# A stick-breaking attention layer: pairs of steps, 64-row tiles on TensorE, and subtractions moved to GpSimd

## What is computed

```python
h = rmsnorm(x, a_norm)                      # x: 2048 x 1024, float32
q, k, v, g = split(h @ w_in, 4)             # 16 heads of 64
z = q @ k.T / 8                             # t x s, only s < t counts
w[t, s] = sigmoid(z[t, s]) * prod(1 - sigmoid(z[t, j]) for s < j < t)
x = x + ((w @ v) * silu(g)) @ w_out
out = rmsnorm(x, final_norm)
```

## Time and profile before

| | us |
|---|---|
| median of 3 runs (1651.22 to 1652.89) | 1651.32 |
| the profiled execution | 1651.07 |
| its span, first to last instruction | 1649.3 |

### The profile page before, as it was taken

The page is one execution under the profiler, slowest core; times in us unless marked ns, Lnnn a source line. Parts: engine busy times, 40 slices in busy tenths (PEclk is TensorE's granted clock), DMA queues, the critical chain, the costliest instruction groups (busy, mean ns, idle before and its releaser), DMA issues.

```text
span 1649.3 us, 23497 instructions
## 1 busy us (share of the span) xinstructions
PE 1638.1 (99%) x8642; PEld 1376.1 (83%) x8642; DVE 1348.6 (82%) x1901; ACT 904.7 (55%) x1782; POOL 165.5 (10%) x200
## 2 busy tenths in 40 slices
PE   9999999999999999999999999999999999999998
PEld 7888878888888888888888888888888888888887
DVE  5536369989898999899998999898889899957874
ACT  6625245655665566656565655656566656743221
POOL 0020020110111011101110211012011101000000
PEclk9999999999999999999999999999999999999999
DMA  9858643343424252434333333425242424779722
GB/s 314 276 163 277 190 142 108 110 126 92 150 68 136 69 154 80 132 94 124 109 98 106 120 113 90 132 87 147 58 147 81 144 77 129 247 259 363 247 105 87
DMA packets 164370, 237.10 MB, mean 144 GB/s; under 512 B 49952, under 2 KB 91936, under 8 KB 164256
## 3 DMA queue, kind: packets, MB, share of 16 engines
q1 hardware_dynamic: 94912, 160.29, 31.5%
q10 hardware_dynamic: 69344, 75.32, 14.6%
HBM read 155.78 MB, written 79.76 MB: 143 GB/s over the span
## 4 chain that ended last, share of the span: by engine, by line
PE 96%; DMA 2%; ACT 1%; DVE 0%; POOL 0%; issue 0%; SPq 0%; DVEq 0%
PE proj_ps L764 31%; PE turn_ps L794 15%; PE o_ps L810 8%; PE o_ps L812 8%; PE z_ps L784 8%; PE z_ps L782 8%; PE proj_ps L713 5%; PE turn_ps L851 3%; PE o_ps L713 3%; PE turn_ps L713 3%; PE z_ps L851 3%; PE proj_ps L851 2%; PE o_ps L851 1%; DMA gate<-gate_cols 1%; POOL w_raw L697 0%; DMA w_raw<-in_w_qkg 0%
## 5 line engine op out<-in xcount | busy, mean ns | idle before, releaser
L1003 ACT ACTIVATE u<-z_ps 128x512 f32<-128x512 f32 (+3 forms) x640 | 341.6, 534 | 365.4 <-PE z_ps L784 362.3
L1236 DVE TENSOR_TENSOR_SCAN u<-u,u 128x512 f32<-128x512 f32 x384 | 492.1, 1281 | 0.0
L1241 DVE TENSOR_TENSOR r_turned_lo<-turn_ps,r_turned_hi 128x512 fp32r<-128x512 f32 (+3 forms) x640 | 380.9, 595 | 103.5 <-ACT r_turned_hi L1009 99.5
L1009 ACT ACTIVATE r_turned_hi<-turn_ps 128x512 fp32r<-128x512 f32 (+3 forms) x640 | 341.0, 533 | 96.7 <-PE turn_ps L794 45.2
L794 PE MATMUL turn_ps<-ident,u 128*128 128x128 f32 x2176 | 352.6, 273 | 0.0
L764 PE MATMUL proj_ps<-hT_hi,w_hi 128*128 128x512 f32 x768 | 317.9, 414 | 0.0
L764 PE MATMUL proj_ps<-hT_hi,w_lo 128*128 128x512 f32 x768 | 317.7, 414 | 0.0
L764 PE MATMUL proj_ps<-hT_lo,w_hi 128*128 128x512 f32 x768 | 317.5, 413 | 0.0
L794 PEld LDWEIGHTS turn_ps<-ident,u 128*128 128x128 f32 x2176 | 266.8, 140 | 54.5
L697 POOL TENSOR_SCALAR w_raw<-w_raw,a_norm_col 128x128 f32<-128x128 f32 x192 | 163.7, 871 | 1201.3 <-DMA w_raw<-in_w_qkg 1201.3
L784 PE MATMUL z_ps<-k_parts,q_swapped 128*128 128x512 f32 (+3 forms) x640 | 235.8, 368 | 0.0
(11 more groups left out here) (138 smaller groups left out, 1601.1 us busy)
## 6 DMA issues: line engine op xcount, KB each, us to landing
qk_hi_cols<-made_hi ACTq DMA_DIRECT2D x64, 256.0 KB, 2.8
qk_lo_cols<-made_lo ACTq DMA_DIRECT2D x64, 256.0 KB, 2.7
x_T<-in_xT SPq DMA_DIRECT2D x29, 512.0 KB, 6.0
w_raw<-in_w_qkg SPq DMA_DIRECT2D x24, 512.0 KB, 3.7
x_rows<-in_x SPq DMA_DIRECT2D x16, 512.0 KB, 4.9
v_rows<-v_stage ACTq DMA_DIRECT2D x32, 256.0 KB
v_here<-v_rows SPq DMA_DIRECT2D x64, 128.0 KB, 3.1
v_next<-v_rows SPq DMA_DIRECT2D x64, 128.0 KB, 3.5
```

Source lines behind the costliest of these rows:

```text
L1003: nc.scalar.activation(u_t[(m // CB) % RU][STEPS[m][3]][:, 0:w], z_ps[m % RZ][:, 0:w], ACT.Sigmoid, scale=-Z_SCALE).then_inc(s_u, 1)
L1009: nc.scalar.activation(rt_hi[m % RT][:, 0:w], t_ps[m % RT][:, 0:w], ACT.Copy).then_inc(s_hi, 1)
L1236: nc.vector.tensor_tensor_scan(u, u, other, start, ALU.mult, op).then_inc(s_r, 1)
L1241: nc.vector.tensor_tensor(rt_lo[m % RT][:, 0:w], t_ps[m % RT][:, 0:w], as_f32(rt_hi[m % RT][:, 0:w]), ALU.subtract).then_inc(s_lo, 1)
```

## The change

It leaves the work of the three stages and its arithmetic as it was, apart from the scores (below), and alters the loop:

- Every engine walks the steps in pairs (`PAIR = 2`); the leads are 10 for scores, 2 for turns and low parts, 8 for scans.
- `scores` makes both steps of a pair with three matmuls each (high by high, low by high, high by low) over 64 rows; the even step uses partitions 0 to 63 and the odd one 64 to 127, in turn. q and k are held in high and low tensors of their own, k twice (once in each half), q with its even blocks in the lower and its odd blocks in the upper half.
- `turn` transposes every 128 x 128 block as two 64 x 128 ones, one from each half, into the two banks of one tensor `turn_ps`, which holds both steps of a pair. It waits until the low parts of the pair before are made.
- `hi` and `lo` read the two banks with a strided pattern. Both wait for the whole pair; `hi` of the odd step also waits on a new semaphore `s_w`, which `weigh` of the even step raises, since there are three `r_turned` buffers.
- PE's order in a pair is turns, scores, weighing of the even step, projections, weighing of the odd step.
- `dif`, `dv_low` and `weight_lo` are on GpSimd; its products with the gain and its low parts of weights are spread over the steps in four parts each.
- The output staging tile `o_stage` is single.

```diff
+PAIR = 2
+LEAD_SCORES = 10
 LEAD_TURN = 2
-LEAD_SCAN = 6
-RU, RZ, RT, RO, RP = 3, 2, 3, 2, 2
+LEAD_SCAN = 8
+RU, RZ, RT, RO, RP = 3, 2, 3, 1, 2
...
+                    for tile, src in ((k_hi, qk_hi), (k_lo, qk_lo)):
+                        sp.dma_start(as_f32(tile[0:HALF, cols]), src[rows, cols]).then_inc(s_k[j], 16)
+                        sp.dma_start(as_f32(tile[HALF:P, cols]), src[rows, cols]).then_inc(s_k[j], 16)
 
...
+                    for tile, src in ((q_hi, qk_hi), (q_lo, qk_lo)):
+                        blocks = src[rows, cols].rearrange("p (i two t) -> p two i t", two=PAIR, t=P)
+                        for odd in range(PAIR):
+                            here = as_f32(tile[c % 2][odd * HALF:(odd + 1) * HALF, :]).rearrange("p (i t) -> p i t", t=P)
+                            sp.dma_start(here, blocks[:, odd]).then_inc(s_q[c % 2], 16)
 
...
+                def weight_lo(t, ks):
+                    if ks.start == 0:
+                        pool.wait_ge(s_whi, t + 1)
+                    for k in ks:
+                        last = nc.gpsimd.tensor_tensor(w_lo[t % 2][:, k, :], w_raw[t % 2][:, k, :],
+                                                       as_f32(w_hi[t % 2][:, k, :]), ALU.subtract)
+                    if ks.stop == KT:
+                        last.then_inc(s_wlo, 1)
+
+                def dif(h, j):
+                    d = NC * h + j
+                    pool.wait_ge(s_va[d % 2], 32 * (d // 2 + 1))
+                    nc.gpsimd.tensor_tensor(va[d % 2][:], vb[d % 2][:], va[d % 2][:], ALU.subtract).then_inc(s_dif, 1)
+
+                def dv_low(h, j):
+                    d = NC * h + j
+                    pool.wait_ge(s_dhi, d + 1)
+                    blocks = slice(j * CB, (j + 1) * CB)
+                    nc.gpsimd.tensor_tensor(dv_head[:, blocks, DH:P], va[d % 2][:], as_f32(dv_head[:, blocks, 0:DH]),
+                                            ALU.subtract).then_inc(s_dlo, 1)
+
...
+                for n in range(-LEAD_SCORES, NS):
+                    if n in PAIR_DIF:
+                        dif(*PAIR_DIF[n])
+                    if n in PAIR_LO:
+                        dv_low(*PAIR_LO[n])
+                    for p in range(PARTS):
+                        ks = range(p * KT // PARTS, (p + 1) * KT // PARTS)
+                        if n - 2 - p in LOAD_W:
+                            weight_normed(LOAD_W[n - 2 - p], ks)
+                        if n - 7 - p in LOAD_W:
+                            weight_lo(LOAD_W[n - 7 - p], ks)
 
...
-                def scores(m, first):
+                def scores(m):
+
                     h, c, j, r = STEPS[m]
-                    lo = score_cols(m)
-                    tau = slice(r * P, (r + 1) * P)
-                    sig = slice(j * CH + lo, (j + 1) * CH)
-                    out = z_ps[m % RZ][:, 0:CH - lo]
-                    if first:
-                        if c == 0 and r == 0:
-                            pe.wait_ge(s_k[j], 32 * (h + 1))
-                        if j == c and r == 0:
-                            pe.wait_ge(s_q[c % 2], 64 * (2 * h + c // 2 + 1))
-                        if m >= RZ:
-                            pe.wait_ge(s_u, m - RZ + 1)
-                        nc.tensor.matmul(out, q_parts[c % 2][:, tau], k_parts[:, sig], start=True, stop=False)
-                    else:
-                        nc.tensor.matmul(out, q_swapped[c % 2][:, tau], k_parts[:, sig], start=False, stop=True).then_inc(s_z, 1)
-
-                def turn(m, blocks):
+                    if c == 0 and r == 0:
+                        pe.wait_ge(s_k[j], 64 * (h + 1))
+                    if j == c and r == 0:
+                        pe.wait_ge(s_q[c % 2], 64 * (2 * h + c // 2 + 1))
+                    if m >= RZ:
+                        pe.wait_ge(s_u, m - RZ + PAIR)
+                    tau = slice(r // PAIR * P, (r // PAIR + 1) * P)
+                    for n, (a, b) in enumerate(((q_hi, k_hi), (q_lo, k_hi), (q_hi, k_lo))):
+                        for odd in range(PAIR):
+                            rows = slice(odd * HALF, (odd + 1) * HALF)
+                            lo = score_cols(m + odd)
+                            sig = slice(j * CH + lo, (j + 1) * CH)
+                            last = nc.tensor.matmul(z_ps[(m + odd) % RZ][:, 0:CH - lo], a[c % 2][rows, tau], b[rows, sig],
+                                                    start=(n == 0), stop=(n == 2))
+                            if n == 2:
+                                last.then_inc(s_z, 1)
+
+                def turn(m):
+
                     _, c, j, _ = STEPS[m]
                     r = sigma_block(m)
                     unit = (m // CB) % RU
-                    if blocks.start == 0:
-                        pe.wait_ge(s_r, m - m % CB + CB)
-                    for t in blocks:
+                    pe.wait_ge(s_r, m - m % CB + CB)
+                    if m and m % PAIR == 0:
+                        pe.wait_ge(s_lo, m)
+                    for t in range(turn_width(m) // P):
                         lo = t * P if j == c else 0
-                        last = nc.tensor.transpose(t_ps[m % RT][:, t * P:(t + 1) * P],
-                                                   u_t[unit][t][:, r * P - lo:(r + 1) * P - lo], ident[:])
-                    if blocks.stop == turn_width(m) // P:
-                        last.then_inc(s_t, 1)
-
-                def weigh(m, first):
+                        for half in range(2):
+                            rows = slice(half * HALF, (half + 1) * HALF)
+                            at = m % PAIR * PAIR * P + t * HALF
+                            last = nc.tensor.transpose(turn_ps[:, half, at:at + HALF],
+                                                       u_t[unit][t][rows, r * P - lo:(r + 1) * P - lo], ident[rows, rows])
+                    last.then_inc(s_t, 1)
+
+                def weigh(m):
                     h, c, j, r = STEPS[m]
                     w = turn_width(m)
+                    if c == 0 and r == 0:
+                        pe.wait_ge(s_dlo, NC * h + j + 1)
                     begin, end = j == c and r == 0, j == NC - 1 and r == CB - 1
+                    if begin and NC * h + c:
+                        pe.wait_ge(s_ost, NC * h + c)
+                    pe.wait_ge(s_lo, m + 1)
                     weights = dv_head[:, j * CB + sigma_block(m), :]
-                    if first:
-                        if c == 0 and r == 0:
-                            pe.wait_ge(s_dlo, NC * h + j + 1)
-                        if begin and NC * h + c:
-                            pe.wait_ge(s_ost, NC * h + c)
-                        pe.wait_ge(s_lo, m + 1)
-                        nc.tensor.matmul(o_ps[:, 0:w], weights, rt_hi[m % RT][:, 0:w], start=begin, stop=False)
-                        return
+                    nc.tensor.matmul(o_ps[:, 0:w], weights, rt_hi[m % RT][:, 0:w], start=begin, stop=False)
                     last = nc.tensor.matmul(o_ps[:, 0:w], weights, rt_lo[m % RT][:, 0:w], start=False, stop=end)
-                    if end:
+                    if m % PAIR == 0:
+                        last.then_inc(s_w, 1)
+                    elif end:
                         last.then_inc(s_o, 1)
                     elif j == c and r == CB - 1:
                         last.then_inc(s_dvused, 1)
-
...
+                for n in range(-LEAD_SCORES, NS, PAIR):
+                    if inside(n + LEAD_TURN):
+                        if n + LEAD_TURN == 0:
+                            pe.wait_ge(s_vT, 1)
+                        turn(n + LEAD_TURN)
+                        turn(n + LEAD_TURN + 1)
                     if inside(n + LEAD_SCORES):
-                        scores(n + LEAD_SCORES, True)
-                        if turned and narrow_scores(n + LEAD_SCORES):
-                            turn(n + LEAD_TURN, range(0, 1))
-                            done = 1
-                        scores(n + LEAD_SCORES, False)
-                    if turned and not narrow_weights(n):
-                        turn(n + LEAD_TURN, range(done, turned))
-                        done = turned
-                    project(filled(n - 1), filled(n))
-                    put_out(out_filled(n - 1), out_filled(n))
+                        scores(n + LEAD_SCORES)
                     if inside(n):
-                        weigh(n, True)
-                        if done < turned:
-                            turn(n + LEAD_TURN, range(0, 1))
-                        weigh(n, False)
-                        if done < turned:
-                            turn(n + LEAD_TURN, range(1, turned))
+                        weigh(n)
+                    project(filled(n - 1), filled(n + 1))
+                    put_out(out_filled(n - 1), out_filled(n + 1))
+                    if inside(n):
+                        weigh(n + 1)
...
                 def hi(m):
-                    w = turn_width(m)
-                    act.wait_ge(s_t, m + 1)
```

(12 more changed lines are left out.)

172 lines of the change are left out of this document (79 added, 93 removed).

## The result

| | before | after |
|---|---|---|
| median of 4 runs each, us | 1651.63 (1651.22 to 1652.89) | 1748.62 (1744.42 to 1750.85) |
| the profiled execution | 1651.07 | 1744.42 |
| its span | 1649.3 | 1742.7 |

The ratio of times is 1.0586 [1.0572, 1.0599]: 97 us slower, where 25 us faster was forecast. *Before* and *after* name the two kernels from here on.

The account below looks back on a forecast made before the run. It took PE's own matmul cadences as the bound (77.7 us a head). From 1651 us it took 51 for tiles and ring, added 14 for late scans and 12 for late GpSimd: 1626 us, range 1572 to 1720.

Parts of the forecast that it names:

- The round trip: PE going into 64-row tiles and back once a pair: 0.19 us taken between 0 and 0.30, 3.8 us more a head.
- PE's own sum: TensorE's work for one head of 20 pairs: 77.7 us before the change, 72.0 after it.
- The gains: Halves side by side on PE: scores 3.3 us less a head, transposes 6.2 less at 0.063 us a block.
- The ring: Turns, scores, even weighing, odd high part, both low parts: 3.92 us a full pair against PE's 3.85; 74.5 a head.
- the first made_low term: VectorE's made_low ahead of its scans ends them 0.37 us late: 14 us given back, bounds 0 and 34.
- GpSimd: Subtractions moved there may come late, so ScalarE and then PE wait: 12 us added, bounds 0 and 60.
- C: Rival: weight loads of the two halves don't overlap, transposes 0.126 us a block, full 0.30 trip; 1749 us, chance 0.15.
- D: Rival: round trip of 0.30 us in the ring and GpSimd late with differences; 1668 us, chance 0.18.
- E: Rival: the halves don't run side by side on PE at all, 19.9 us more a head; 1970 us, chance 0.05.
- B: Rival: changing tiles is almost free, PE 68 us a head, the ring 72.2; 1583 us, chance 0.18.
- the cadences: PE's matmul spacing before: 0.23, 0.18, 0.12 and 0.07 us for 512, 384, 256 and 128 columns.
- the loads of q and k: 128 more k loads and q in 128-column blocks, hidden by earlier loading: free; 1 or 2 us a head if not.

Follow-up runs that it names:

- e2: The kernel after with the even step weighed ahead of the turns instead of behind the scores; 1712.21 us, 1.0376 of before.
- e5: e2 with successive query chunks' outputs in two banks in turn, the second being a spare one; 1679.41 us, 1.0166 of before.
- e9: e5 with each low part's store issued in the pair that makes it, not a pair later; 1656.79 us, 1.0039 of before.
- e11: The kernel after with only the store of each low part issued in the pair that makes it; 1725.51 us, 1.0448 of before.
- e12: e9 with 4.8 projection matmuls a head moved into the pairs that begin the diagonal units of chunks 1 to 3; 1644.37 us, 0.9963 of before.
- e8: e5 with scores and turns both back in 128-row tiles, so no change of tile height; 1706.05 us, 1.0334 of before.
- e1: The kernel after with `dif`, `dv_low` and `weight_lo` back on VectorE at the steps of before; 1761.75 us, 1.0676 of before.
- e4: The kernel before with only the GpSimd moves (three subtractions, multiplication in parts); 1653.15 us, 1.0016 of before.
- e10: e5 with two projection matmuls of each pair put between turns and scores, one more round trip a pair; 1766.51 us, 1.0698 of before.

## Why the prediction was wrong

The 97 us, taken away step by step, each measured by a run: weighing ahead of turns -36 (e2), a second output bank -33 (e5; this wait exists only once the weighing is moved), stores at once -23 (e9, and e11 alone), projections moved -12 (e12). That is 104, and ends 7 below before. The steps build on each other, so another order would divide them otherwise.

*The round trip, taken as 0.19: the first step that failed.* Rows 4 said 0.30 for one, and I went below them because "nothing says 64-row tiles pay all of it". Measured: 0.15 in, 0.23 out, and 0.05 for a load of fp32r weights between turns and scores, which the sum didn't have at all: 0.43. With 20 trips a head that is 8.6 us instead of 3.8, so PE's own sum is 77.7 - 3.3 - 6.4 + 8.6 = 76.6, not 72.0. The gains were sized right (0.061 a block for 0.063, couples at 0.23); their price was not. Of 9.7 us saved a head, 1.1 stay, 18 us in all by this sum, 27 by e8 less e5. The prediction did give the dearer row as 20 us in its text, and then chose against its own nearest row.
The Trainium skill, "TensorEngine Tiling (Array Packing)", Key Properties, says that changing the mode drains TensorE and that tiles load and multiply in parallel. Both halves agree with the traces here: idle loads of 0.35 to 0.37 us at a change, and a couple of loads in 0.061 us, of matmuls in 0.23.

*The ring, taken as 3.92: the step that cost most.* It has a median of 4.30. Term by term: second weighing matmul at 1.77 behind the turns' first load instead of 1.56 (way out and exposed loads, +0.21); weighing's end to the odd high part 0.10 instead of 0.04 (+0.06); low parts +0.04; last low part to the next load 0.11 instead of 0.05 (+0.06), and 0.01 from rounding. Sum 0.38. Over all places of a head the pairs' medians sum to 81.1 us where 74.5 was predicted: 6.6 x 16 = 106 us, nearly the whole miss of 123. And because the ring, not PE, set the end in full pairs, the trip's way in was free there (PE waits anyway), but the way out lay in the ring. The prediction named the ring, its members and the wait, and charged 2.5 us a head for it (74.5 against PE's 72.0); what failed is the length of its terms: the way out (0.14 taken, 0.23 measured), the exposed loads, and the handoffs, of which only the one from ScalarE to VectorE came from a row. A ring of 3.92 against 3.85 is the bound already, and every term that is a little larger goes into the time in full.

*Stores: a queue that the prediction missed.* It asked whether scans fit behind `made_low`, and never what `made_low` itself waits for. ScalarE issues stores one step later in before and a pair later in after. In the example the store was issued 9 us after the only `made_lo` tile was full, and the landing came on top. Such waits grew from 3.4 us to 21.0 in VectorE's rows and cost 23 us of time (e11). The row before, then the two after:

```profile
DVE made_lo L1222 <- DMA qk_lo_cols<-made_lo: 3.4, 1, 3.4
...
DVE made_lo L1260 <- DMA gate_cols<-made_lo: 11.2, 3, 5.3
DVE made_lo L1262 <- DMA qk_lo_cols<-made_lo: 9.8, 5, 5.8
```

Together with the first made_low term (14 us) and GpSimd (12), 26 us had stood for all disturbance of single pairs, and 35 were measured: the size was not far off, its cause was another.

*GpSimd: the sign was wrong.* 12 us were added for being late; e1 shows that the move gives 13 in this ring, since VectorE is in it. Bounds of 0 and 60 excluded a gain, without a reason from a row. In the kernel before, where VectorE isn't in the bound, it costs 2.7 (e4). Its work was also taken too dear: on average 0.67 us for 128 columns of two inputs and 0.98 for 256, 247 us in all instead of 390 to 780. The rows after:

```profile
L722 POOL TENSOR_TENSOR w_lo<-w_raw,w_hi 128x128 fp32r<-128x128 f32 x192 | 121.8, 666 | 149.2 <-ACT w_hi L1010 149.2
...
L736 POOL TENSOR_TENSOR dv_head<-v_here,dv_head 128x256 fp32r<-128x256 f32 x64 | 62.7, 981 | 298.4 <-ACT dv_head L1004 298.4
```

The Trainium skill, "SBUF — State Buffer", Who interferes with whom, lets such pieces and VectorE's scans lock each other out. The traces agree, and both sides are longer where they meet. In these rows GpSimd's first five pieces run beside low parts and its last two beside two scans; the last row is a pair of scans with no such work beside it:

```profile
734.93 2.12 POOL L722 TENSOR_TENSOR w_lo<-w_raw,w_hi 128x128 fp32r<-128x128 f32 x5
...
736.96 3.21 DVE L1276 TENSOR_TENSOR_SCAN u<-u,u 128x512 f32<-128x512 f32 x2
...
737.72 2.71 POOL L722 TENSOR_TENSOR w_lo<-w_raw,w_hi 128x128 fp32r<-128x128 f32 x2
...
741.27 2.44 DVE L1276 TENSOR_TENSOR_SCAN u<-u,u 128x512 f32<-128x512 f32 x2
```

A piece takes 0.42 us in the first row and 1.36 in the third; the two scans beside it take 3.21 instead of 2.44. Over the whole run a piece of 128 columns has a median of 0.46 us and a longest of 1.51, and scans take 30 us longer in after than in e1 (13 in the wide ones, 1303 against 1269 ns, and 17 in those of `unbroken`, 883 against 816). Rows 8, with a GpSimd instruction of one input, had shown 0.05 us, and the sum went by that. It is a real cost, but VectorE's busy time still falls, from 1346.4 us in e1 to 1308.2, and e1 shows that the move pays.

*The rivals.* C (loads of the halves one after the other) stood at 1749, which is the time measured. Its mechanism is refuted: a block costs 0.061, under its own deciding point of 0.08. That its number came true is luck; only the dear round trip, one of its parts, was right. Nor does the number follow from its terms as written: 77.7 - 3.3 + 2.3 + 6.0 is 82.7 us a head, 1731 us in all; the 83.8 holds 1.1 more that its text doesn't derive. D (ring longer, GpSimd late, 1668) had the right place and one wrong half; its text works out 55 us for GpSimd and adds 35. E (no overlap) is refuted by the couples, two matmuls in 0.23 us, and B (free change of tiles) by e10. The rival that was missing is the true one: halves in parallel, but a full-price trip in a ring without slack.

What was right: where the time is bound before, the cadences, that couples run side by side, the loads of q and k at nothing (PE waits for none of them in after), and that relieving VectorE is worth nothing where PE is the bound (e4). Of the signs that it named, the cadence of couples and blocks and the new wait came (the two of a couple start 0.03 us apart, not a few ns); the full pair (4.30, not 3.9 to 4.1), the weighing's gap (0.23, not 0.15 to 0.2), VectorE (40 us less, not 80) and GpSimd (398 us, not 500 to 900) did not.

## What to carry to other kernels

When an order is changed, write the new ring down term by term and compare it with the bound's own sum; if it is within a few per cent, count it as the bound and look for the instruction in it that can be issued earlier: here one `weigh` moved up gave 36 us, though it brought a new wait for the single output bank. Where an array mode makes work cheaper, charge its way in and out once for each visit, and put all the work that gains by it into one visit. For each waiting instruction on an engine of the ring, ask what frees its tile, and when that store is issued.

## What the runs showed of the hardware

- Changing between 128-row and 64-row tiles and back costs TensorE about 0.43 us here: 0.15 in, 0.23 out, 0.05 in between for the first fp32r load (0.38 to 0.46 by the pairs of e5 to e8); a further trip costs 0.35 in full pairs (e10). The load is not done ahead at a change (idle 0.35 to 0.37 us before it), while between matmuls of one height it is (rows 2 and 3).
- Two 64-row tiles load weights and multiply at the same time, the second mostly some 0.03 us behind the first: 0.061 us for a couple of 64 x 128 float32 blocks with 64 moving columns, where a 128 x 128 block takes 0.109; 0.23 us for a couple of 512-column matmuls. The number is the same as for a sixteen-row block.
- In the full pair shown, 0.11 us pass from VectorE's last low part to PE's next load, 0.10 from the modelled end of PE's matmul to ScalarE's start, 0.03 from ScalarE's end to VectorE's start.
- GpSimd subtracts 128 float32 columns in 0.46 us (median), 256 in 0.74; beside a scan of VectorE a piece of 128 took 1.36, and the two scans 0.77 us longer. The means, 0.67 and 0.98, hold both cases.
- PE waited from 1478.8 to 1484.9 us, and from 1481 to 1488 its granted clock was 0.52; with the waits shortened (e9), the clock from 1400 to 1500 us is 0.98 instead of 0.93.
